# Two transformer blocks on one core: in the output and down projections the weights' high part meets both parts of the activations in one 512-column matmul

## What is computed

```python
# first block, one layer
merged = (g[:, :, 0] * (ya @ w_branch_a[l]) + g[:, :, 1] * (yb @ w_branch_b[l])
          + g[:, :, 2] * (yc @ w_branch_c[l]))
x = x + merged @ w_out[l]                               # output projection, 1024 x 1024
h = rms_norm(x, norm_ffn_g[l])
u = causal_dwconv(h @ ffn_up[l], ffn_conv_w[l], ffn_conv_b[l])
u_gate, u_val = jnp.split(u, 2, axis=-1)
x = x + (jax.nn.gelu(u_gate) * u_val) @ ffn_down[l]     # down projection, 2816 x 1024
...
# second block, each of two layers
mix = jnp.einsum('bsd,de->bse', merged, w_o)
x = layer_norm(ALPHA * x + mix, ln1_g, ln1_b)
up = causal_dwconv_2(jnp.einsum('bsd,df->bsf', x, w_up), ffn_conv_w)
a, b = jnp.split(up, 2, axis=-1)
ffn = jnp.einsum('bsf,fd->bsd', jax.nn.silu(a) * b, w_down)
x = layer_norm(ALPHA * x + ffn, ln2_g, ln2_b)
```

## Time and profile before

| | before |
|---|---|
| median of 3 runs | 1310.39 us |
| lowest, highest | 1307.92, 1311.63 us |
| profiled execution, its own time | 1314.53 us |
| its span, first to last instruction | 1312.7 us |
| TensorE matmuls (PE) | 1263.2 us busy, 96% of the span, 10288 instructions |
| TensorE weight loads (PEld) | 1222.0 us busy, 93%, 10288 instructions |
| VectorE (DVE) | 870.1 us busy, 66% |
| ScalarE (ACT) | 710.6 us busy, 54% |
| GpSimd (POOL) | 354.0 us busy, 27% |
| mean granted TensorE clock | 0.985 of full speed |

### The profile page before, as it was taken

The page is one execution under the profiler, slowest core; times in us unless marked ns, Lnnn a source line. Parts: engine busy times, 40 slices in busy tenths (PEclk is TensorE's granted clock), DMA queues, the critical chain, the costliest instruction groups (busy, mean ns, idle before and its releaser), DMA issues. The chain is left out here.

```text
span 1312.7 us, 27372 instructions
## 1 busy us (share of the span) xinstructions
PE 1263.2 (96%) x10288; PEld 1222.0 (93%) x10288; DVE 870.1 (66%) x1469; ACT 710.6 (54%) x1235; POOL 354.0 (27%) x345
## 2 busy tenths in 40 slices
PE   9999879799999999999998999999999989999997
PEld 8988779789999999998998999999988989999997
DVE  4756667567777764665576877755765587777655
ACT  3655457445566654555544666644555444666643
POOL 1021100732343421130035433413220045344313
PEclk9999889999999999999999999999999998999998
DMA  6634344456466666444455466665444554566662
GB/s 221 196 115 129 97 119 131 137 181 190 147 193 190 193 193 190 150 150 134 153 170 161 129 189 187 195 186 174 132 143 136 170 161 129 164 191 192 182 196 87
DMA packets 60288, 212.70 MB, mean 162 GB/s; under 512 B 6688, under 2 KB 7968, under 8 KB 60064
## 3 DMA queue, kind: packets, MB, share of 16 engines
q1 hardware_dynamic: 60192, 211.39, 52.6%
HBM read 210.31 MB, written 1.05 MB: 161 GB/s over the span
## 5 line engine op out<-in xcount | busy, mean ns | idle before, releaser
L989 PE MATMUL bank<-xhi,whi 128*128 128x256 f32 x2368 | 676.5, 286 | 22.8 <-DVE wlo L1293 14.5
L1293 DVE TENSOR_TENSOR wlo<-raw,whi 128x1024 fp32r<-128x1024 f32 (+1 forms) x400 | 493.9, 1236 | 295.2 <-ACT whi L665 293.6
L990 PE MATMUL bank<-xlo,whi 128*128 128x256 f32 x2368 | 661.9, 280 | 0.0
L991 PE MATMUL bank<-xhi,wlo 128*128 128x256 f32 x2368 | 661.8, 279 | 0.0
L665 ACT ACTIVATE whi<-raw 128x1024 fp32r<-128x1024 f32 (+1 forms) x400 | 415.6, 1040 | 147.5 <-PE bank L991 139.4
L989 PEld LDWEIGHTS bank<-xhi,whi 128*128 128x128 f32 x2368 | 451.0, 190 | 42.0 <-DVE wlo L1293 18.4
L990 PEld LDWEIGHTS bank<-xlo,whi 128*128 128x128 f32 x2368 | 449.5, 190 | 0.7
L991 PEld LDWEIGHTS bank<-xhi,wlo 128*128 128x128 f32 x2368 | 449.3, 190 | 0.0
L577 POOL TENSOR_TENSOR fprod<-ugate,uval 128x256 f32<-128x256 f32 x66 | 97.9, 1483 | 222.5 <-DVE uval L1630 216.9
L989 PE MATMUL bank<-fhi,whi 128*128 128x256 f32 x528 | 148.8, 282 | 0.8 <-POOL flo L566 0.6
L991 PE MATMUL bank<-fhi,wlo 128*128 128x256 f32 x528 | 148.2, 281 | 0.0
(11 more groups left out here) (201 smaller groups left out, 1336.7 us busy)
## 6 DMA issues: line engine op xcount, KB each, us to landing
raw<-in_w_win SPq DMA_DIRECT2D x140, 512.0 KB, 3.5
raw<-in_w_up SPq DMA_DIRECT2D x132, 512.0 KB, 3.6
raw<-in_w_down SPq DMA_DIRECT2D x48, 448.0 KB, 3.5
raw<-in_w_merge SPq DMA_DIRECT2D x32, 512.0 KB, 4.2
raw<-in_w_out SPq DMA_DIRECT2D x24, 512.0 KB, 3.6
raw<-in_w_down SPq DMA_DIRECT2D x24, 512.0 KB, 3.5
x<-in_x SPq DMA_DIRECT2D x4, 256.0 KB, 3.6
rgw<-in_rg_w SPq DMA_DIRECT2D x1, 1024.0 KB, 9.9
```

Of the source, the lines that this page charges most:

```text
L989: pe.matmul(ps, whi[:, slot, w], hi, start=first, stop=False)
L990: pe.matmul(ps, whi[:, slot, w], lo, start=False, stop=False)
L991: return pe.matmul(ps, wlo[:, slot, w], hi, start=False, stop=last)
L1293: dve.tensor_tensor(wlo[:, n % RING, w], raw[:, n % RING, w], whi[:, n % RING, w].bitcast(f32), ALU.subtract) \
```

## The change

Every block of wout and down is now two matmuls. One takes `whi` and 512 columns, the activations' hi and lo next to each other, and writes all 512 columns of the bank: the left half gets hi x hi, the right half hi x lo. The second takes `wlo` and the 256 columns of hi, and adds into the left half. For this `xhi` and `xlo` become the two halves of one tensor `xsplit` (tile by tile, hi then lo), and `fhi` and `flo` those of `fsplit`; the names stay as views, and whoever writes or reads them does so as before. The residual has a second step on VectorE: it waits for the first (new semaphore `res_half`) and adds the right half; `res_new` is counted up only then. The win, merge and up stages keep three matmuls for a block.

```diff
-        xhi = sb("xhi", [P, KT, S], r32)
-        xlo = sb("xlo", [P, KT, S], r32)
+        xsplit = sb("xsplit", [P, KT, 2, S], r32)
+        xhi, xlo = xsplit[:, :, 0, :], xsplit[:, :, 1, :]
...
-        fhi = sb("fhi", [P, FT, S], r32)
-        flo = sb("flo", [P, FT, S], r32)
+        fsplit = sb("fsplit", [P, FT, 2, S], r32)
+        fhi, flo = fsplit[:, :, 0, :], fsplit[:, :, 1, :]
...
+            def wide_product(bank, slot, block, split, first, last):
+
+                w = slice(block * P, (block + 1) * P)
+                pe.matmul(bank[:], whi[:, slot, w], split.rearrange("p a s -> p (a s)"), start=first, stop=False, skip_group_check=True)
+                return pe.matmul(bank[:, 0:S], wlo[:, slot, w], split[:, 0, :], start=False, stop=last, skip_group_check=True)
...
             def wout(name, base, which):
                 for t in range(KT):
                     r = RESULT[name] + t
-                    plain(START[name] + t, r, bank_of(r)[:, 0:S], ready=[(m_lo, base + k + 1) for k in range(KT)] if t == 0 else None)
+                    n = START[name] + t
+                    begin(n, r)
+                    for k in range(KT):
+                        if t == 0:
+                            pe.wait_ge(m_lo, base + k + 1)
+                        mm = wide_product(bank_of(r), n % RING, k, xsplit[:, k, :, :], k == 0, k == KT - 1)
+                    mm.then_inc(unit_done, 1)
...
                     for k in range(DOWN_PARTS[part]):
-                        mm = product_of(down_bank(name, t)[:, 0:S], n % RING, k, fhi[:, k0 + k, :], flo[:, k0 + k, :],
-                                        k0 + k == 0, k0 + k == FT - 1)
+                        mm = wide_product(down_bank(name, t), n % RING, k, fsplit[:, k0 + k, :, :], k0 + k == 0, k0 + k == FT - 1)
...
                 dve.scalar_tensor_tensor(tile(x, t, it, tiles), tile(x, t, it, tiles), alpha, as_tile(bank[:, 0:S]), ALU.mult, ALU.add) \
-                    .then_inc(res_new, 1)
+                    .then_inc(res_half, 1)
+                wait(dve, res_half, RES[which] + t + 1, it, tiles)
+                dve.tensor_tensor(tile(x, t, it, tiles), tile(x, t, it, tiles), as_tile(bank[:, S:2 * S]), ALU.add).then_inc(res_new, 1)
```

More of the change, by code:

```diff
@@ L1602, in merge, with residual @@
                 split(KT - 1)
-            def residual(name, t, n, alpha, bank, it=0, per=0, tiles=0):
+            def residual(which, t, n, alpha, bank, it=0, per=0, tiles=0):
                 wait(dve, unit_done, n + 1, it, per)
                 dve.scalar_tensor_tensor(tile(x, t, it, tiles), tile(x, t, it, tiles), alpha, as_tile(bank[:, 0:S]), ALU.mult, ALU.add) \
-                    .then_inc(res_new, 1)
+                    .then_inc(res_half, 1)
+                wait(dve, res_half, RES[which] + t + 1, it, tiles)
+                dve.tensor_tensor(tile(x, t, it, tiles), tile(x, t, it, tiles), as_tile(bank[:, S:2 * S]), ALU.add).then_inc(res_new, 1)
             def wout(name, which, alpha):
@@ L1615, in wout @@
                             deviation(which, u)
-                    residual(name, t, START[name] + t, alpha, bank_of(RESULT[name] + t))
+                    residual(which, t, START[name] + t, alpha, bank_of(RESULT[name] + t))
                 if which in LNI:
@@ L1642, in body @@
                             deviation(which, KT - 2)
-                        residual(name, t, n, alpha, down_bank(name, t), it, 6, 2)
+                        residual(which, t, n, alpha, down_bank(name, t), it, 6, 2)
                 repeat(dve, name, DOWN, 6, body, peel_first=True)
```

2 lines of the change are left out of this document (1 added, 1 removed).

## The result

| | before | changed |
|---|---|---|
| median | 1311.65 us (6 runs) | 1320.08 us (6 runs) |
| lowest, highest | 1307.92, 1314.38 us | 1317.51, 1323.69 us |
| ratio of the two | | 1.0056, 95% interval 1.0031 to 1.0080 |
| profiled execution, its own time | 1314.53 us | 1319.91 us |
| its span | 1312.7 us | 1318.1 us |

The changed kernel is slower by 0.6%, where 1300.0 us and a gain of 0.8% were forecast; the time lies above the range of 1292 to 1309 us.

The account below looks back on a forecast made before the run. The prediction took TensorE's matmul pace, set by weight loads, as the bound: 13.5 us saved by wide matmuls less 3.1 us for VectorE's second step gave -10.4 us, from 1310.39 to 1300.0 us, range 1292 to 1309 us.

Parts of the forecast that it names:

- What bounds the kernel: Wout and down stages go at TensorE's pace; TensorE has a matmul under way in 96% of the span.
- The price of the wide matmul: In wout and down, 215 to 217 ns for 512 columns, a block 331 ns, saving 13.5 us.
- the gates' rows: Recurrence's plain f32 matmuls, taken as streaming 213.3 ns each with 4 ns extra; the model for a wide matmul.
- the fast pace: Narrow matmul starts 113.3 ns apart, 340 ns a block; assumed for 150 of the 720 blocks before.
- the load is the bound, and the columns hide behind it: A weight load costs 111 to 113 ns, over 106.7 ns for 256 columns; load-bound case 0.60, 1300.0 us.
- The lower bound of the block: 324 ns for columns and 2 ns each; the upper, 353 ns, if a wide matmul costs two narrow ones.
- the columns themselves are slow, and the pace goes slow: Rival, chance 0.10: wide matmul 235 ns, nothing saved, 3.1 us for VectorE plus 2.0 us for pace; 1315.5 us.
- The second step: VectorE's added residual step costs 0.52 us at each of six stage ends, 3.1 us; 42 inside stages cost nothing.
- one more or one less fall, 1.7 us either way: Clock falls around the waits of wout20 and wout21 might shift; 1.7 us put into the range, not the sum.
- The spread from unedited stages: Win, merge and up stages may change pace; nothing expected on balance, 4 us allowed.
- the slow pace: Narrow matmuls 117.7 ns apart, 353 ns a block; assumed for 570 of the 720 blocks before.
- Feed and layout: Faster down units still get their weights in time, and the tensors' new layout changes no transfer size; both cost nothing.

Follow-up runs that it names:

- the packed bf16: Changed kernel with down1 on bf16 weights and moving bf16 numbers two bytes apart, down20 and down21 on other operands; 1309.19 us beside 1313.99, down1 325 ns a block.
- the layout alone: Kernel before with only the two-part tensors, three narrow matmuls and one residual step kept; 1313.20 us beside 1313.80, ratio 0.9993.
- halves: Changed kernel with the wide matmul cut into two of 256 columns, both residual steps kept; 1319.66 us beside 1313.80, ratio 1.0055.
- one step: Changed kernel with wide matmuls but without the residual's second step, so weights' hi times activations' lo is left out; 1315.11 us, ratio 1.0009.
- three steps: Changed kernel with one more dependent VectorE step in each residual, changing nothing in x; 1331.48 us, ratio 1.0125 to the kernel before.
- the kernel with the last tile narrow: Changed kernel with three narrow matmuls and one residual step in each wout and down stage's last tile; 1313.54 us beside 1313.99, ratio 0.9997.
- the changed kernel's second execution: Changed kernel unaltered, run again on the same chip with a second trace; 1317.16 us over 12 runs, ratio 1.0040 to the kernel before.

## Why the prediction was wrong, point by point

**What bounds the kernel: right.** The stages go at TensorE's pace, and ScalarE waits for it before and after. (A slip in the working: 61.9 us for 528 matmuls are 117.2 ns each and not 117.5. The sum used 353 ns for a block, and that is what the stage's starts give.)

**The price of the wide matmul: wrong, and this step alone takes the gain away.** The prediction put it at 215 to 217 ns from the gates' rows; it is 235 ns, and 225 to 231 ns in the few blocks that catch the fast pace. A block was to fall from 340 or 353 to 331 ns and is 353. The measured load floor of 111.7 ns is what the earlier trace rows gave. The step that failed is the one behind it, "the load is the bound, and the columns hide behind it": from two prices that are nearly equal nothing says which of them sets the distance. 512 columns of fp32r cost twice 113 ns or more with the load hidden, and with loads of half the recorded length a block still takes 340 ns. So 256 columns cost 113 ns by themselves, the load of 111.7 ns lay in their shadow from the beginning, and there was nothing to take away. That the gates' rows did not carry over has a likely reason, which no run here tests: they spend the time of 512 columns on 256, so their operand may be read half as fast, and how the operand is read has a price here (216 and 226 ns by spacing alone). The lower bound of the block, 324 ns, is what the packed bf16 has (325 ns), the upper one, 353 ns, what the fp32r has.

**The pace.** In the kernel before, wout1 went at the fast pace, 340 ns. fp32r stages with wide blocks had 353 ns in every execution seen, but for at most six blocks of a stage, all in its first third. In the profiled executions wout1 lost 0.7 us by it (21.9 to 22.6). This was the rival "the columns themselves are slow, and the pace goes slow", with its 235 ns and its 353 ns. It had 0.10, because the earlier trace rows stood against it. It named the mechanism on TensorE, and its loss of 5.1 us lies among the measured 5 to 7; it made that up of 3.1 us for the second step and 2.0 us for the pace. The runs put most of the loss on the step: without wide matmuls it is as large (1.0055), and with them but without the step at the ends there is none that can be told (1.0009 and 0.9997). The 2.0 us for the pace are neither shown nor refuted by these times, whose intervals are 2 to 3 us either way. The traces speak for a loss of about that size: the six edited stages together took 266.0 to 267.9 us in the three traces with narrow blocks (before, the layout alone, halves), and 267.7 to 268.8 us in the four with wide ones throughout (the changed kernel twice, one step, three steps).

**The second step: the price about right, the consequence underrated.** It puts 0.45 us into the norm's chain (1304.59 - 1304.14), where 0.52 was taken. How much that is by itself is seen where none of the five stretches has a lower clock. Their sums in two such traces, of the kernel with the last tile narrow and of the changed kernel's second execution:

```profile
sum 39.35, PE 37.19 PEld 34.08 DVE 28.33 ACT 18.62 POOL 18.69; mean PE 7.44 PEld 6.82 DVE 5.67 ACT 3.72 POOL 3.74
```

```profile
sum 41.24, PE 37.65 PEld 34.28 DVE 30.43 ACT 18.63 POOL 18.72; mean PE 7.53 PEld 6.86 DVE 6.09 ACT 3.73 POOL 3.74
```

These are 1.9 us for five ends, and with the 0.4 us from down21's last matmul to the end (14.21 against 13.77 us) 2.3 us for six, instead of 3.1. The 42 inside the stages cost nothing that shows, as forecast: the last residual begins 0.32 us behind the last matmul in wout20 of the changed kernel as in that of the kernel before. But what the six cost in all is the difference between a ratio of 1.0040 to 1.0056 and one of 0.9997, 5 to 7 us. The prediction let the clock stand in its range at "one more or one less fall, 1.7 us either way", as if the sign were open. On balance it is a loss. An estimate of what the clock takes is the span times one less the mean clock: 19.6 us in the mean of 35 runs of the kernel before, 21.5 us in the changed kernel's second set of 12 runs, 21.8 us in the kernel with halves (two steps), 20.1 us in the one with wide matmuls and one step, and 29.7 us with three. So about 2 us of the changed kernel's loss go to the clock, give or take 1 us. A single execution doesn't have to show it: in seven traces with two steps nine of the 35 norm stretches had a fall, in five with one step three of 25, and such a fall made a stretch 0.7 to 1.1 us longer. With three steps it was all five of the one trace. The changed kernel's second trace had no fall at a norm and was as long as the first (1320.77 and 1319.91 us).

**The spread from unedited stages: right in kind.** Their pace is drawn anew in each execution. The up1 stage is the same code in the kernel with the layout alone and in the one with halves, and these are their rows, in that order.

```profile
346.46:471.05 124.59, 124.46 (x1056) 124.26 (x1057) 98.19 (x140) 82.89 (x134) 49.34 (x43) 1.00 0.59 177
```

```profile
343.07:463.43 120.36, 120.24 (x1056) 120.04 (x1057) 93.12 (x139) 81.50 (x134) 47.40 (x43) 1.00 0.61 183
```

That is 4.2 us for one stage at full clock (and up21 of the changed kernel took 121.8 and 124.9 us in its two profiled executions), which is the 4 us that the prediction allowed. The kernel before alone ran from 1306.66 to 1320.22 us in 35 runs, so one profiled execution says nothing of a half per cent, and the prediction's correction from 1314.53 to the median was no more than a draw. That all three down stages of the profiled execution were slow was in part a draw too: in the kernel with halves down1 took 60.6 us with narrow matmuls at the fast pace, though the other eight narrow down stages of three traces were slow in all or most of their blocks. So the 13 ns of the slow pace are not bound to the stage.

**Feed and layout: right**, both at nothing.

**What stays open**: what draws the pace, and why wide matmuls bring the slow one within a block or two. And the sum of the loss: 2.3 us of steps and about 2 us of clock leave 1 to 3 of the 5 to 7 us, of which the lost fast pace may be up to 2; the runs are too few to separate these, and the step's influence on the pace of the stage behind it can't be excluded.

## What to carry to other kernels

Joining two matmuls that use the same weights pays only if the weight load lasts longer than the columns, so measure both alone: shorten the columns until the distance stops falling, and compare the floor with the full one. Take a rate for streamed columns only from matmuls with the same operand type and spacing. A dependent step ahead of a norm costs itself and, in some executions, the clock behind it; inside a stage it is free only while its engine still needs less for a tile than TensorE (some 2.55 us against 2.83 in wout20 of the changed kernel; 3.25 with three steps, and it was late). Where a step can be spared at the last tile alone, that is the tile to spare it at.

## What the runs showed of the chip that I had not expected

- At full clock 512 columns take 216 ns as bf16 two bytes apart, 226 ns as bf16 four bytes apart, and as fp32r 225 to 231 ns for a few blocks and 235 ns from then on. The three-part products read at four bytes as well: 113.3 ns for 256 columns at the best, where 109 ns were measured for packed bf16.
- At half clock the surcharge is gone. TensorE's timeline of the changed kernel in wout21, where the granted clock is 1.2 GHz:

```profile
1088.95 0.63 PE L996 MATMUL bank<-xsplit,whi 128*128 128x512 f32 x1
1089.38 0.41 PE L997 MATMUL bank<-xsplit,wlo 128*128 128x256 f32 x1
```

  The distance is 0.43 us, and 512 columns at 1.2 GHz are 427 ns.
- The slow pace looks like a constant of 13.3 ns on a block and not like a rate: 340 to 353 ns for 768 columns in three matmuls, 353 in two, and 466.7 ns for 1024 (an estimate at the fast rate is 453.3, and 13.3 more). No stage of bf16 showed it.
- With weights of 128 x 128 numbers of four bytes, matmuls follow each other no closer than 111.7 ns in the mean, the same for 128, 192 and 224 columns; with bf16 weights 109 ns were seen.
- The same VectorE step over 128 x 256 numbers, SBUF to SBUF (line 1623 in the kernel with three steps), took 0.42 us 37 times and 0.95 to 1.02 us 11 times.
